# x loaded first, the bias table written later, and the stage boundaries worked through by PSUM banks and by token halves, in a two-block transformer kernel

## What is computed

```python
def first_block(x, c, ...):
    mod = silu(c) @ ada_w + ada_b                      # 6 vectors of 2048: sh1, sc1, g1, sh2, sc2, g2
    h = rms_norm(x, mix_pre_g) * (1 + sc1) + sh1
    proj = h @ w_in                                    # q, k, v (8 heads of 128), a, g
    attn = causal attention of q, k, v
    u = silu(layer_norm(causal_depthwise_conv(a * sigmoid(g), 31 taps)))
    y = concatenate([attn, u]) @ w_out
    x = x + g1 * rms_norm(y, mix_post_g)
    h = rms_norm(x, ffn_pre_g) * (1 + sc2) + sh2
    y = (silu(h @ w_gate) * (h @ w_up)) @ w_down       # inner width 5632
    return x + g2 * rms_norm(y, ffn_post_g)

def second_block(x, c, ctx, c_ctx, ...):
    sh1, sc1, g1, sh2, sc2, g2 = split(silu(c) @ w_ada + b_ada); csh1, csc1 likewise from c_ctx
    h  = rms_norm(x) * (1 + sc1) + sh1
    hc = rms_norm(ctx) * (1 + csc1) + csh1
    y = neighbourhood attention, 16 heads, of h over h and hc, with a relative bias rpb, @ w_o
    x = x + g1 * y
    h = rms_norm(x) * (1 + sc2) + sh2
    gate, up = split(dwconv3(h @ w_up))                # inner width 5504
    return x + g2 * ((silu(gate) * up) @ w_down)
```

## Time and profile before

| | |
|---|---|
| three runs | 2684.46, 2671.09, 2674.61 us; median 2674.61 |
| profiled execution | 2671.1 us, of which the span from the first to the last instruction is 2669.5 |
| PE busy | 2579.2 us, 97% of the span |
| PE loading weights | 2128.9 us, 80% |
| DVE, ACT, POOL busy | 69%, 49%, 5% |
| mean DMA rate | 233 GB/s over the span; 323 to 386 in the first tenth |

### The profile page before, as it was taken

One profiled execution on the slowest core, in us unless ns is written; L12 is line 12 of the kernel. 1 busy time (PEld: TensorE's weight loads), 2 busy tenths in 40 slices (PEclk: granted clock), 3 DMA queues, 4 the chain that ended last, 5 costly groups with the idle time before them and its releaser, 6 DMA issues.

```text
span 2669.5 us, 38377 instructions
## 1 busy us (share of the span) xinstructions
PE 2579.2 (97%) x13324; PEld 2128.9 (80%) x13324; DVE 1836.8 (69%) x2256; ACT 1303.3 (49%) x1864; POOL 137.6 (5%) x237
## 2 busy tenths in 40 slices
PE   6999798999999999999899999999999999999999
PEld 3687687788788888888787878787788888888887
DVE  2349678787888686888755556655578876667565
ACT  2349555554344344465625242424466555565453
POOL 2112011000200000000001000100000000000000
PEclk8999899999999999999999999999999999999999
DMA  9989676689888687789354545454568855556554
GB/s 323 386 314 371 189 276 215 244 304 342 281 295 276 225 288 250 244 311 314 122 191 142 190 136 193 142 189 138 163 232 283 283 184 186 182 172 206 194 192 163
DMA packets 236156, 622.94 MB, mean 233 GB/s; under 512 B 20140, under 2 KB 24535, under 8 KB 231120
## 3 DMA queue, kind: packets, MB, share of 16 engines
q1 hardware_dynamic: 212832, 523.30, 58.5%
q0 software_dynamic: 22144, 91.84, 10.1%
q10 hardware_dynamic: 1072, 6.35, 0.6%
HBM read 613.80 MB, written 7.60 MB: 233 GB/s over the span
## 4 chain that ended last, share of the span: by engine, by line
PE 88%; DVE 4%; DMA 4%; ACT 2%; issue 2%; ACTq 0%; POOL 0%; DVEq 0%; SPq 0%; POOLq 0%
PE ps L2136 12%; PE ps L2081 11%; PE ps L2085 11%; PE ps L2083 11%; PE ps L2475 8%; PE ps L2477 8%; PE ps L2479 8%; PE ps L2138 6%; PE ps L2117 2%; PE ps L2119 2%; PE ps L2121 2%; DMA raw<-in_w_in 1%; PE ps L2407 1%; DMA slot<-in_ada_w 1%; PE ps L2396 1%
## 5 line engine op out<-in xcount | busy, mean ns | idle before, releaser
L1291 DVE TENSOR_TENSOR w_lo<-raw,w_hi 128x1024 fp32r<-128x1024 f32 x766 | 932.1, 1222 | 606.3 <-ACT w_hi L730 604.0
L730 ACT ACTIVATE w_hi<-raw 128x1024 fp32r<-128x1024 f32 x766 | 809.6, 1059 | 1005.9 <-PE ps L2085 378.6
L2136 PE MATMUL ps<-h_both,w_hi 128*128 128x512 f32 x1376 | 482.6, 395 | 0.0
L2081 PE MATMUL ps<-w_hi,h_both 128*128 128x512 f32 x1152 | 465.6, 404 | 12.1 <-DVE h_both L1364 7.2
L2085 PE MATMUL ps<-w_hi,h_both 128*128 128x512 f32 x1152 | 452.0, 392 | 0.0
L2083 PE MATMUL ps<-w_lo,h_both 128*128 128x512 f32 x1152 | 451.3, 392 | 0.0
L2138 PE MATMUL ps<-h_both,w_lo 128*128 128x256 f32 x1376 | 385.8, 280 | 0.0
L2136 PEld LDWEIGHTS ps<-h_both,w_hi 128*128 128x128 f32 x1376 | 258.0, 187 | 60.9 <-issue 0.2
L1298 DVE SCALAR_TENSOR_TENSOR acc<-ada,cact,acc 128x1024 f32<-128x1024 f32 x224 | 291.6, 1302 | 8.6 <-DMA ada<-in_w_ada 5.4
L2475 PE MATMUL ps<-w_hi,f_hi 128*128 128x512 f32 x696 | 272.1, 391 | 2.0 <-DVE f_lo L1568 1.4
L2479 PE MATMUL ps<-w_hi,f_lo 128*128 128x512 f32 x696 | 271.8, 390 | 0.0
(11 more groups left out here) (266 smaller groups left out, 3127.8 us busy)
## 6 DMA issues: line engine op xcount, KB each, us to landing
ada<-in_w_ada SPq DMA_DIRECT2D x192, 512.0 KB, 4.3
raw<-in_ffn_w_up SPq DMA_DIRECT2D x160, 512.0 KB, 4.5
slot<-in_ada_w POOLq DMA_DIRECT2D x60, 1024.0 KB, 9.2
raw<-in_na_w_qkv SPq DMA_DIRECT2D x96, 512.0 KB, 4.7
raw<-in_w_gate SPq DMA_DIRECT2D x88, 512.0 KB, 4.9
raw<-in_w_up SPq DMA_DIRECT2D x88, 512.0 KB, 4.8
raw<-in_w_down SPq DMA_DIRECT2D x88, 512.0 KB, 5.3
raw<-in_ffn_w_down SPq DMA_DIRECT2D x86, 512.0 KB, 4.6
```

What stands on the lines that cost most here:

```text
L730: act.activation(w_hi[:, s, :], raw[:, s, :], ACT.Copy).then_inc(hi_ready, 1)
L1291: dve.tensor_tensor(w_lo[:, s, :], raw[:, s, :], w_hi[:, s, :].bitcast(F32), ALU.subtract).then_inc(lo_ready, 1)
L2081: pe.matmul(o, hi_[:, k, a], wh, start=(k == 0), stop=False)
L2136: pe.matmul(ps[:, 4 * part + g, :].rearrange("p (a n) -> p a n", a=2), w_hi[:, s, a], h_both[:, :, k, :], start=(k == 0), stop=False)
```

## The change

It has these parts:

1. **x first.** SP issues the DMA of x ahead of the first four groups (it was the last of ACT's). ACT squares the first token half ahead of the silu. SP's waits for `group_done` ahead of a tile are written anew and are the same for tiles 4 to 19; tile 20 waits for group 31 in place of 28. The picking of the shift columns begins 10 matmuls later in its tile.
2. **Bias table later.** The 8 table writes are issued after group 58, and not before tile 55 has been used, that is at the start of attention 1a.
3. **Layer norm.** The mean is subtracted one tile earlier, the table of the root is loaded earlier, PE sums the squares ahead of output tile 0, and two `scale_unit` are taken out of this place and done beside the last two output tiles.
4. **Boundaries by banks and tokens.** In `last_rows` the last two tiles are taken bank by bank, and a semaphore tells each bank; ACT and DVE work on y bank by bank (512 columns each). `rows` takes 2 column blocks a step where it opens a boundary and 2 blocks of both token halves later on (10 steps in place of 8).
5. **Down-projection 1** finishes its last eight tiles (`LAST`) in token order, not the last four; the last four have buffers of their own (`last_hi`, `last_lo`, `last_f_hi`, `last_f_lo`), the first two steps of `rows` run inside the pass for t=0, and `hi` of the next four tiles need not wait for the last four. The streams of SP, ACT and DVE are written out without a loop for its second half, and the 26 `unit` that lay beside the tiles 44 to 87 lie beside 44 to 77.
6. **Feed-forward 2.** The first two `rows` steps run inside the pass for t=0, and tiles 0 and 1 are multiplied for t=1 first and for t=0 after that.
7. **End.** The second half of the last x is made and sent in two parts.

```diff
+            sp.dma_start(x[:, :, :], ins["x"][0].rearrange("(t p) d -> p t d", p=P)).then_inc(x_landed, 16)
             for g in range(4):
...
-                if g == 57:
+                if g == 58:
                     pool.wait_ge(table_landed, 16 * H2)
+                    pool.wait_ge(tile_used, T_AG + RING + 56)
...
+        ROWS_TURN = (((1,), 0, 2), ((1,), 2, 2), ((1,), 4, 4), ((0,), 0, 2), ((0,), 2, 2), ((0,), 4, 4),
+                     *((BOTH, k, 2) for k in range(8, KD, 2)))
+        ROWS_WIDE = (((1,), 0, 2), ((1,), 2, 2), ((0,), 0, 2), ((0,), 2, 2), *((BOTH, k, 2) for k in range(4, KD, 2)))
+        def rows_done(order, j, ts):
+            return 1 + max(s for s, (st, k0, nk) in enumerate(order) if set(st) & set(ts) and k0 <= 2 * j < k0 + nk)
+        LAST = 2 * RING
...
+            def last_rows(T, n, operands, between=iter(()), beside=lambda step: None):
+                steps_ = [*(((j,), (0, 1)) for j in range(n - 2)), ((n - 2, n - 1), (0,)), ((n - 2, n - 1), (1,))]
                 for t in (1, 0):
+                    for step, (js, cs) in enumerate(steps_):
+                        for j in js:
+                            wh, wl, fh, fl, F = operands(j)
+                            if t and 0 in cs:
+                                pe.wait_ge(flo_ready, F + 1)
+                                pe.wait_ge(lo_ready, T + (j + 1 + RING))
+                            mm = row_product(wh, wl, fh, fl, 1, False, j == n - 1, (t,), cs=cs,
+                                             between=between if j > 1 or t == 0 else iter(()))
+                            if t == 0 and 1 in cs:
+                                mm.then_inc(tile_used, 1)
+                        if step >= n - 2 and (t or 0 in cs):
+                            mm.then_inc(part_done, 1)
                         if t == 0:
+                            beside(step)
...
+            def out_turn(n, phase, Tend, bufs, n0, m_, scale):
 
-                dve.wait_ge(later_done, phase + 1)
                 dve.wait_ge(half_read, 2 * phase + 2)
-                dve.wait_ge(y_read, 2 * phase + 1)
-                gated(1, scr)
+                y_gated(phase, 1, 0, bufs[1])
                 r = rows_rstd(n)
-                part(1, 0, r)
-                part(1, 1, r)
+                part(1, 0, r, bufs)
+                y_gated(phase, 1, 1, bufs[1])
+                part(1, 1, r, bufs)
+                lo(Tend, 0)
+                scale()
+                y_gated(phase, 0, 0, bufs[1])
+                make_diag(n + 1, 1)
+                r = rows_rstd(n + 2)
+                y_gated(phase, 0, 1, bufs[1])
+                rows(0)
+                part(0, 0, r, bufs)
+                part(0, 1, r, bufs)
+                lo(Tend, 1)
+                rows(1)
+                make_diag(n + 3, 0)
...
+            def boundary(T, m_, xn, n0):
...
+                def y_was_read(g):
+                    if g == 2:
+                        pe.wait_ge(x_ready, 2 * PH_OUT2 + 2)
+                tile(0, (1,))
+                tile(1, (1,))
+                more(2)
+                more(3)
+                tile(0, (0,))
+                more(4)
+                tile(1, (0,))
+                more(5)
+                for j in range(2, 6):
+                    tile(j, BOTH)
+                    more(4 + j)
...
+            def down_turn(T, target, m_, xn, n0, between, beside):
...
+                more(2)
+                tile(0, (1,))
+                tile(1, (1,))
+                between()
+                tile(2, (1,))
                 more(3)
-                between()
-                for j in range(RING):
-                    tile(j, (0,))
-                    more(4 + j)
-                for j in range(RING, CT):
-                    tile(j, range(NT))
+                more(4)
+                tile(3, (1,))
+                more(5)
+                tile(0, (0,))
+                tile(1, (0,))
+                more(6)
+                tile(2, (0,))
+                more(7)
+                tile(3, (0,))
+                more(8)
...
-            turn(T_QKV2, (*lat, 2, USE2["qkv2"]), M["lat"], 4, 16, b_g1_sums, ctx_rows)
+            down_turn(T_QKV2, (*lat, 2, USE2["qkv2"]), M["lat"], 4, 18, b_g1_sums, ctx_rows)
```

More of the change, by code:

```diff
@@ L978, in turn @@
-                y_stat(n + 2, 0, phase)
+                y_stat(n + 2, phase, 0, Tend)
+                rows(0)
                 hi(Tend, 1)
-                rows(0)
+                rows(1)
+                x_first(phase, 0)
+                x_stat(n + 3, phase, 0)
+                rows(2)
+                rows(3)
+                hi(Tend, 2)
+                rows(4)
+                hi(Tend, 3)
+                for j in range(4, 9):
+                    rows(j + 1)
+                    hi(Tend, j)
@@ L1643, in boundary @@
                 make_diag(n, 1)
                 lo(Tend, 0)
+                update(0, 0, phase, Tend, scr)
+                rows(0)
+                update(0, 1, phase, Tend, scr)
+                rows(1)
+                lo(Tend, 1)
                 make_diag(n + 1, 0)
-                lo(Tend, 1)
+                rows(2)
+                rows(3)
                 lo(Tend, 2)
-            def turn(n, phase, Tend, bufs, n0, m_, after=lambda: None, beside=lambda n: None):
-                gy, scr = bufs
-                def part(t, half, r):
-                    xt = x[:, t, half * TILE:(half + 1) * TILE]
-                    dve.scalar_tensor_tensor(out=xt, in0=(gy, scr)[half][:, t, :], scalar=r, in1=xt, op0=ALU.mult, op1=ALU.add)\
-                        .then_inc((x_half, x_ready)[half], 1)
+                for j in range(3, 9):
+                    rows(j + 1)
+                    lo(Tend, j)
@@ new lines, in boundary, with y_gated, part @@
+                clear(acc0)
+                for j in range(9, CT + 3):
+                    lo(Tend, j)
+            def y_gated(phase, t, c, scr):
+                dve.wait_ge(y_read, 2 * NT * phase + part_of(t, c))
+                gated(t, c, scr)
+            def part(t, half, r, bufs):
+                xt = x[:, t, half * TILE:(half + 1) * TILE]
+                dve.scalar_tensor_tensor(out=xt, in0=bufs[half][:, t, :], scalar=r, in1=xt, op0=ALU.mult, op1=ALU.add)\
+                    .then_inc((x_half, x_ready)[half], 1)
@@ L1686, in turn @@
+                y_gated(phase, 0, 1, bufs[1])
+                r = rows_rstd(n + 2)
+                part(0, 0, r, bufs)
+                part(0, 1, r, bufs)
+                rows(2)
+                lo(Tend, 3)
+                make_diag(n + 3, 0)
+                rows(3)
+                rows(4)
+                for j in range(4, 9):
+                    rows(j + 1)
+                    lo(Tend, j)
                 after()
@@ L1706, in _ @@
             out_tile(T_OUT1, F_OUT1, ORDER1, BESIDE)
-            for u in range(2):
-                scale_unit(SC2_LN + u)
             dve.wait_ge(tr_free[1], M["ln"] + 1)
@@ L2179, in rows @@
             def rows(m_, s_, order, xn):
[L2181 to L2182 removed]
+                (ts, k0, nk), b = order[s_], 1 - s_ % 2
+                pe.wait_ge(xn_ready, xn + 2 - ts[0])
                 bank_free(b, m_ + s_ // 2)
[L2184 to L2187 removed]
@@ L2464, in _, with row_product @@
                     attention(0, M["att1a"], NT, qkv_written, lambda u: columns_tile(T, 3 * CT, u, 2, USE2["q1"] + 1))
-            def row_product(T, s, fh, fl, half, first, last, ts, hold=None, between=iter(())):
+            def row_product(wh, wl, fh, fl, half, first, last, ts, hold=None, between=iter(()), cs=range(2)):
                 for t in ts:
```

558 lines of the change are left out of this document (331 added, 227 removed), and 6 rows, old and new, of the table act_step.

## The result

The changed kernel's median is 2664.47 us over 18 runs (2659.91 to 2672.45). The kernel before, run 18 times in all beside it, has 2681.01 us (2671.09 to 2690.23), not the 2674.61 us of the first three runs. The ratio is 0.9945, 95% interval [0.9932, 0.9957]: 14.7 us faster, or 16.5 us by the difference of the medians. Forecast were 2645 us and a gain of 27.3 us. The time lies above the range's top of 2660, the sign is right, and the gain is a little over half of the forecast.

A forecast was written before the change was run, and what follows sets the result against it. PE was taken as the bound, busy 2579.2 of 2669.5 us. Terms 6 + 9 + 0 + 3 + 6 + 2 + 1.3 = 27.3 off 2671.1 gave 2643.8, put at 2645 us for the runs' median; range 2632 to 2660.

The forecast's parts named there:

- The base: Whole kernel: gains taken from the profiled 2671.1 us, and the runs' median put 3.5 us above that execution.
- x first: Start: x lands sooner, the DMA's hole fills, tile 20 behind group 31 frees 1.35 us; gain 6 us, ends 3 and 8.
- Bias table: Table writes moved beside attention 1a: pause on v falls from 11.6 to about 2 us; gain 9, ends 0 and 11.6.
- rival 1: Attention: the table's writes stall it, half to all of the 9 us lost; 2648 to 2656 us, chance 0.15.
- Layer norm and its two units: Layer norm gains 3.5 us, the units moved to output projection 1's end give 3.5 back; net 0, ends +3.5 and -2.
- rival 5: Boundaries and attention: several short pauses, each followed by 3 us at half speed costing 1.5; slower, about 2685 us, chance 0.04.
- Boundary after output projection 1: Work in 512-column parts shortens 7.9 us of idle and half speed, second tile waits instead; gain 3, ends 0 and 6.
- Down-projection 1: Its end: the chain of about 8 us fits into 10.9 us of t=0 work; gain 6, ends 2 and 11.
- Feed-forward 2: Its start: 5 us of pause go, half tiles cost 1.8 and new waits 1.2; gain 2, ends -1 and 5.
- End: Last product and sum fall from 1.23 to 0.69 us each, last DMA halves; gain 1.3, ends 0.5 and 2.
- Rival 2: Start: x delays the groups, its term becomes 0 to -5; gain 16 to 21, 2650 to 2658 us, chance 0.12.
- Rival 3: Boundaries: nearly all idle goes and layer norm gains 3.5; gain 34 to 45, 2626 to 2637 us, chance 0.12.

The follow-up runs named there:

- run 18: Not a label but part of "run 18 times in all": the kernel before, unchanged, run 18 times beside the changed kernel; median 2681.01 us.
- sums_later: `tile20_sooner` with the scale's column sums taken only in the pass for t=0, the units left at the end; 2653.19 us, ratio 0.9905.
- units_back: Changed kernel with the two scale units done behind the layer norm again; 2662.29 us, ratio 0.9935.
- table_early: Changed kernel with the table writes behind group 57 again, without their wait; 2673.03 us, ratio 0.9973.
- tile20_sooner: Changed kernel with tile 20 waiting for group 28, as before, and not for group 31; 2660.08 us, ratio 0.9924.
- x_late: `tile20_sooner` with x as ACT's last DMA again and squared after the silu; 2665.74 us, ratio 0.9960.
- ff2_whole: Changed kernel with feed-forward 2's tiles 0 and 1 multiplied whole; 2670.64 us, ratio 0.9971.
- the fourth: Fourth trace of the kernel before, no edit; a single execution of 2679.97 us.
- units_att: `tile20_sooner` with the two scale units done in the second attention, beside its units 2 and 5; 2650.99 us, ratio 0.9905.
- units_att2: `units_att` once more, no further edit; 2656.17 us, ratio 0.9911.
- again: Second trace of the kernel before, no edit; 2678.40 us (12 runs; the traced one 2669.42), ratio 0.9999.

## Why the prediction was wrong

**The base.** 27.3 us were taken off 2671.1 us, and 3.5 put back for a median of three runs. The median of 18 is 2681.0. With the same sum it would have been 2681 - 27.3 = 2654, inside the range and still 11 us under the measured. The step "the median of the runs was 3.5 us above that execution" failed by 6.4 us: runs of this kernel lie 20 us apart, and three don't fix the middle. What makes the untraced runs of before slower than three of its four traces stays open; it isn't the mean clock.

**x first, forecast 6, measured -0.8.** The sizing of x was right: squares at 9.30 us, transposes at 17.36 against 22.88, DMA share 1.03, and 4 to 6 us in the experiments. The failed step is "Tile 20 behind group 31 takes 0.5 MB, 1.35 us, out of the way of the last groups". I counted a wait as a gift to the queue and did not ask who is late by it. The tile was asked for only after group 31 was used and landed 6.6 us after ACT was ready for it. Behind it in ACT's order stood the sums, for which PE waited 2.46 us, and with tile 20 all later tiles came late.

**Bias table, forecast 9, measured 7.4 in the traces, 7 and 9 in the medians.** The step held. The pause went (11.6 to 1.4 us), and the writes held up raw tiles in attention more than the 0.7 us that I put: tiles 60 to 72 are 2.0 to 2.5 us longer than before (mean 52.9) in the three traces of the changed kernel, 3.8 in `sums_later`; rival 1 in small. The DMA view from 286 to 296 us of the changed kernel:

```profile
q0 software_dynamic: 267, 0.87, 69.3%
q1 hardware_dynamic: 295, 0.55, 20.4%
...
raw<-in_w_in SPq DMA_DIRECT2D x2, 512.0 KB, 12.3
```

SP's queue gets 20% and a tile lands after 12.3 us, between the 22.9 us of the earlier trace rows and the 8 us of an even split. The Trainium skill, page DMA: Bandwidth & Descriptors, section Queues, rings and completion order, lets each engine take turns among its queues packet by packet; the trace agrees that both queues move at once, and doesn't show equal time. Equal shares were my reading; the page has turns by packet.

**Layer norm and its two units, forecast +3.5 - 3.5.** Both halves came: the traces show +4.8 before tile 108, and a stall of 3.4 to 3.5 us for `acc_s`. The failed step is "I give 3.5 back". The stall was priced as idle time only, and where I priced half speed I took 3 us for a stretch, 1.5 us. Here it is about 17 us, 8.5 us lost if all of it runs at half the rate. Counted on the products (matmuls of 512 columns) it is 7.8: from the 60th product before the end of the projection to the wait for the first diagonal the changed kernel takes 29.1 to 30.4 us, `units_back` 18.7, and 3.4 of the difference are the stall. The long stretch is there in all seven traces with the stall (the changed kernel three times, `table_early`, `tile20_sooner`, `x_late`, `ff2_whole`) and in two of eleven without it. `sums_later` takes away the stall alone, and the stretch goes. The two together, 3.4 + 8.5 us less the 0.9 us of the boundary (next paragraph), are 11.0 us. The changed kernel's traces are 11.4 us longer here than the three of before without such a stretch (48.7); the table's 9.7 is less because the fourth has one. So the stall makes the stretch nearly sure, and shorter pauses of 0.9 to 1.5 us at the same place sometimes do it too. That is rival 5's mechanism, at one place and at six times its price. Why pauses of 3.1 us, in `sums_later` of 5.0, in attention 1a are followed by no such stretch stays open.

**Boundary after output projection 1, forecast 3.** `units_back`, free of stall and long stretch, takes 33.3 us from the last output product (503.3) to the end of the eighth chunk tile (536.6), before 35.1 us (513.1 to 548.2). That is 1.8 us, the favourable end. ACT's copy of tile 122, which waits for PE a little behind that point, follows the last output product by 33.5 to 34.8 us in the four traces of before (mean 34.2) and by 32.8 to 34.4 in thirteen with the new boundary (mean 33.3). So the gain is 0.9 us, and the step "I take 3" was three times too large. The pause before the first tile is shorter (1.45 us there, before 3.35), the second tile now waits for more rows, as the step had it.

**Down-projection 1, forecast 6, measured 5.3.** The chain fits into the t=0 pass, the window of 12 us is full. The loss in the t=1 pass is there (1.99 us for `last_f_lo` at 1276 us, 1.06 and 0.91 in the other two traces), and the context's wait stays (PE 6.10 of 8 us).

**Feed-forward 2, forecast 2, measured -0.6.** The mechanism is right and the size off. The idle of 3.45 us became 0.51 + 0.66 + 0.35 + 1.24 = 2.8 us in four waits, where I had put 1.2; the half tiles' 1.8 us came on top (a pair of matmuls takes 0.23 us in a half tile, as forecast, and 0.35 in a whole one). That leaves a gain of 0.4; where the other 1.0 us went no run shows. The half tiles earn their price only against their absence, 2.6 us by `ff2_whole`.

**End, forecast 1.3, measured 1.5.** Each piece takes 0.69 us.

**The rivals.** Rival 2's size came, by luck (a gain of 16 to 21 us was its claim, the medians have 16.5), but not its way: the groups were not delayed, tile 20 was. Rival 1 holds on the mechanism and not on the size: some 2.4 us, where it claimed 4.5 to 9. Rival 3 is refuted at two of three boundaries. Rival 5 is right on the mechanism and, for the whole, on the wrong side of the sum. The last part's claims on squares, transposes and DMA share came as written, and so did the wait of 4.91 us, now 1.47; PE's idle total is 76 us, not 68.

## What to carry to other kernels

Price a new pause on TensorE with what follows it: the same 3.4 us were cheap beside units in attention and cost over three times their length where they broke a full stretch. When a wait is added to protect one stream, find the copy that stands behind it and when its engine will be ready. And take the base from as many runs as there are; cutting several traces at the same tiles shows which terms came and which stretches are chance.

## What was not expected of the hardware

**A stretch at half speed can last 14 to over 18 us with PE busy throughout.** At 494 us PE is busy 16.91 of 17 us at 0.50, in `table_early` all of 18.5 us from 500 us on. Another place is 1584 to 1596 us. Of the eighteen traces four have a wait of 0.94 us before it, and three of them (the first of the changed kernel, `x_late`, `units_att`) such a stretch of 14 us; `units_att2` has the wait alone. The fourteen with a wait of 0.78 to 0.81 us have none. No run here changes that wait by itself, so whether it is the cause stays open.

**The same matmuls ran at two rates at full clock.** From 2230 to 2330 us PE is busy all the time at clock 1.00, and yet the windows of the kernel before (first and again) differ by 12 matmuls:

```profile
2230.00:2330.00 100.00, 100.00 (x567) 86.77 (x567) 63.81 (x77) 58.36 (x66) 0.00 (x0) 1.00 0.60 187
```
```profile
2230.00:2330.00 100.00, 100.00 (x579) 87.45 (x578) 65.11 (x79) 59.43 (x67) 0.00 (x0) 1.00 0.64 190
```

That is 2% and makes 4 us from tile 516 to 762: the table's 675.7 and 675.5 against 671.3 and 671.8. `units_att`, `ff2_whole` and the fourth trace of before had it too, the last one from 2030 to 2130 us (568 in 100 us, before 579). It comes and goes between executions of one kernel; no run here tells why.
